# Products of constants placed in TensorE's waits at the two expert stages' seams

## What is computed

```python
def hierarchical_moe(h, ...):            # 4 groups of 8 experts, the 2 best of the best group
    glog = xf @ w_group + b_group
    g = argmax(glog)
    vals, loc = top_k(elog_g, 2)
    ...
    hb = silu(xb @ w_gate[e]) * (xb @ w_up[e])     # 1024 -> 512, per expert
    return hb @ w_down[e]                          # 512 -> 1024
```

## Time and profile before

| | us |
|---|---|
| median of 3 runs | 1779.08 (1778.0 to 1780.77) |
| the profiled execution's own time | 1777.53 |
| its span, first to last instruction | 1775.6 |
| TensorE busy | 1513.4 (85%), mean granted clock 0.918 |
| VectorE, ScalarE, GpSimd busy | 931.6, 167.4, 111.5 |
| read from HBM | 531.62 MB, 303 GB/s over the span |

### The profile page before, as it was taken

How to read it: one execution, slowest core, us unless ns; L and a number is a source line. 1 busy time by engine, 2 the same in 40 slices (tenths; PEclk the granted TensorE clock), 3 DMA queues, 4 the chain that set the end, 5 groups by cost and what they waited for, 6 DMA issues and landing times. The chain is left out here.

```text
span 1775.6 us, 33411 instructions
## 1 busy us (share of the span) xinstructions
PE 1513.4 (85%) x14935; PEld 1023.3 (58%) x14935; DVE 931.6 (52%) x1904; ACT 167.4 (9%) x389; POOL 111.5 (6%) x120
## 2 busy tenths in 40 slices
PE   8999967787777999776666666789999999999998
PEld 6655534454444995443333333589699446779843
DVE  6754344533235775344212221398867563886756
ACT  3210010000000101000100000111100003400000
POOL 2000100000000530000000000070000001000000
PEclk9999988888888999898878888799999999999999
DMA  9489999999999959999999999925355434345420
GB/s 315 185 322 425 391 417 426 426 426 426 427 426 409 377 210 367 426 422 428 426 427 427 426 428 426 395 95 206 139 190 190 141 123 157 125 142 191 150 88 24
DMA packets 80845, 540.11 MB, mean 304 GB/s; under 512 B 7454, under 2 KB 9566, under 8 KB 54332
## 3 DMA queue, kind: packets, MB, share of 16 engines
q1 hardware_dynamic: 78860, 531.18, 74.3%
q0 software_dynamic: 1808, 6.69, 1.0%
q10 hardware_dynamic: 32, 0.07, 0.0%
HBM read 531.62 MB, written 6.29 MB: 303 GB/s over the span
## 5 line engine op out<-in xcount | busy, mean ns | idle before, releaser
L973 PE MATMUL ps<-ring,work 128*32 128x256 f32 x3584 | 298.9, 506 | 207.4 <-DMA ring<-in_moe_w_up 206.9
L973 PEld LDWEIGHTS ps<-ring,work 128*32 128x32 f32 x3584 | 163.1, 144 | 338.1 <-issue 310.0
L2190 DVE TENSOR_TENSOR rowb<-rowb,ps 128x128 f32<-128x128 f32 x64 | 18.4, 287 | 354.0 <-ACT rowb L1857 353.9
L949 PE MATMUL ps<-ring,work 128*128 128x512 f32 x312 | 139.5, 592 | 0.0
L993 PE MATMUL ps<-ring,multi 128*32 128x256 f32 x1920 | 116.7, 383 | 0.3 <-DMA ring<-in_moe_w_down 0.2
L949 PEld LDWEIGHTS ps<-ring,work 128*128 128x128 f32 x312 | 59.0, 190 | 72.7 <-issue 72.7
L1550 PE MATMUL ps<-hT,ring 128*128 128x128 f32 x768 | 95.4, 275 | 1.5 <-ACT hT L1771 1.5
L949 PE MATMUL ps<-work 128*128 128x512 f32 x212 | 96.0, 592 | 0.0
L1550 PEld LDWEIGHTS ps<-hT,ring 128*128 128x128 f32 x768 | 90.4, 192 | 1.9 <-ACT hT L1771 1.9
L993 PEld LDWEIGHTS ps<-ring,multi 128*32 128x32 f32 x1920 | 62.8, 111 | 43.2 <-issue 2.9
L1014 PE MATMUL ps<-hres,rowb 128*32 128x256 f32 (+1 forms) x1240 | 84.5, 386 | 1.2 <-DVE rowb L2157 1.1
(11 more groups left out here) (624 smaller groups left out, 2268.6 us busy)
## 6 DMA issues: line engine op xcount, KB each, us to landing
ring<-in_moe_w_up SPq DMA_DIRECT2D x62, 2048.0 KB, 23.3
ring<-in_moe_w_gate SPq DMA_DIRECT2D x60, 2048.0 KB, 18.8
ring<-in_moe_w_down SPq DMA_DIRECT2D x58, 2048.0 KB, 24.0
ring<-in_w_ff SPq DMA_DIRECT2D x32, 2048.0 KB, 8.7
ring<-in_sc_w_in SPq DMA_DIRECT2D x6, 2048.0 KB, 22.3
ring<-in_ssm_w_glu SPq DMA_DIRECT2D x4, 2048.0 KB, 17.9
ring<-in_lru_w_in SPq DMA_DIRECT2D x3, 2048.0 KB, 17.6
ring<-in_lru_w_out SPq DMA_DIRECT2D x2, 2048.0 KB, 21.7
```

What stands on the lines that cost most here:

```text
L949: mm = pe.matmul(ps[:, product_bank[n][i], :], left[:, k, :], right[:, k, :], start=(j == 0 and k == 0), stop=(j == pieces - 1 and k == 1))
L973: mm = pe.matmul(ps[32 * q:32 * q + 32, bank, 0:256].rearrange("p (u n) -> p u n", u=2), x[:, k, :], gu[:, k, :, P * q:P * q + P], start=( ...
L2190: link(V.tensor_tensor(hid[b], silu[b], ps[:, 4 + b, P:2 * P], ALU.mult))
```

## The change

`keep_busy` takes a count of columns (288 before) and a bank (5 before). Two calls of 128 columns are added between ranks and picks in both layers; four calls in bank 7 stand between the last expert's gate and up products in layer 1; behind the last combination there are three calls in layer 0 (none before) and five in layer 1 (one before); one call follows the meta tokens' sum (L1366) and one the transposes of block 1 ahead of the wait for `ffn1_taken`. Nothing is removed or moved, and no other engine's program changes.

```diff
-            def keep_busy(n):
+            def keep_busy(n, cols=288, bank=5):
 
                 for _ in range(n):
-                    pe.matmul(ps[:, 5, 0:288], before[:, :], w_route[:, 1, :, :].rearrange("p k n -> p (k n)"), start=True, stop=True)
+                    pe.matmul(ps[:, bank, 0:cols], before[:, :], w_route[:, 1, :, :].rearrange("p k n -> p (k n)")[:, 0:cols],
+                              start=True, stop=True)
...
                 running_ranks(ps[:, 4, 384:384 + nb], tmp_a[:, 64:64 + nb], 1)
+                keep_busy(2, 128)
                 pe.wait_ge(*nth(f"one_hots{l}", 1))
...
                             gate_or_up(xT[b], 4 + b, gu, 0).then_inc(S(f"gate_up{l}"), 1)
+                            if l == 1:
+                                keep_busy(4, bank=7)
                         if gate_ is not None:
...
                 pe.end_ifs()
-                if l == 1:
-                    keep_busy(1)
+                keep_busy((3, 5)[l])
...
             pe.matmul(ps[:, 4, 0:NTAIL], ones[:, :], meta_acc[:, 0, :], start=True, stop=True).then_inc(S("meta_summed"), 1)
+            keep_busy(1)
...
                 transposes("ffn1", [1, 2], "ffn1_normed", only=i, bank=6, left="ffn1_left" if i == 0 else None)
                 if i == 0:
+                    keep_busy(1)
                     pe.wait_ge(*nth("ffn1_taken", 2))
                 s5_inputs(i)
```

## The result

The changed kernel takes **1782.6** against 1778.86 for the kernel before beside it (medians of 10 runs each), a ratio of 1.0024 [1.0016, 1.0032]. A second measurement on another occasion gave 1780.78 against 1778.33, 1.0012 [1.0003, 1.0022]. So it is slower by 2 to 4 us; forecast were 1774.8 and 4.3 gained.

What follows compares the result with a forecast made beforehand. Transfers bound both expert stages; outside them TensorE's lateness goes to the end whole. Gains of 4.06 (layer 1's seam), 0.25 (layer 0) and 0 (picks) sum to 4.3, from median 1779.08 to 1774.8 us; range 1772.6 to 1778.7.

Steps and rivals of the forecast that it cites:

- Five calls behind the last combination: Layer 1, ahead of the transposes: 2.65 us of calls fit in a wait of 4.19 and cost nothing at full clock.
- The clock term of 2.40: Layer 1, transposes to second L1439 group: the clock holds, adding 2.40 us, so the gain grows from 1.66 to 4.06.
- the weakest point: Layer 1, between transposes and L1439: idle 1.5, then 1.7 us, with only 1.6 of products between; the clock must hold.
- rival 1: Clock falls again between layer 1's transposes and L1439: only 1.9 to 3.0 us gained, 1776.1 to 1777.2; chance 0.30.
- The 1.66 ahead of the up products: Layer 1's last up products at full clock; the down matrix's second half, landing late, limits the seam's gain to 1.66 us.
- Layer 0 (0.25): Calls behind layer 0's combination and L1366: 0.25 us gained, at most 0.3, as the third unit's transfer limits it.
- 1.6 in a wait of 2.26: Three calls behind layer 0's last combination: 1.6 us of products hidden in a wait of 2.26.
- The picks (0): Two calls of 128 columns between ranks and picks: 0.5 us of products, hardly delaying the picks; gain taken as 0.
- the bounds of 0 and 1.15: Layer 1's picks: gain between 0 and 1.15 us, the latter if picks take 1.0 instead of 1.93.
- The one on the slow side: Fillers themselves late behind layer 1's last combination and ahead of its up products, if the clock at 1120 is 0.50; chance 0.05.
- the five: The five rivals: clock falls again, picks' filler holds the clock, layer 0 turns against it, fillers late, nothing holds.
- a lucky one: The profiled execution of the kernel before took 1777.53 us, 1.55 under the median of 1779.08.

Runs made afterwards that it cites:

- e9: e7 plus nine calls in the body of layer 1's branch, which is never taken, so every executed product is the same; 1780.83 us, ratio 1.0011.
- e13: The changed kernel without the branch in TensorE's program, all its calls in place; 1777.17 us, ratio 0.9997 to the kernel before.
- e4: The changed kernel with its three and five calls moved from behind the branch to ahead of it; 1777.58 us, ratio 0.9996 to the kernel before.
- e5: e4 without the two calls of 128 columns between ranks and picks; 1776.64 us, ratio 0.9991 to the kernel before.
- e16: e5 measured once more, nothing changed; 1777.05 us, ratio 0.9998 to the kernel before.
- e7: The kernel before with three and five calls behind the branch (before: none and one) as the only change; 1778.48 us, ratio 1.0004.
- e8: The kernel before with three and five calls ahead of the branch and none behind it as the only change; 1778.24 us, ratio 1.0002.
- e6: The kernel before plus only the two calls of 128 columns between ranks and picks; 1778.96 us, ratio 1.0002.
- e10: The changed kernel plus 52 calls inside layer 1's branch, never taken; 1782.36 us, ratio 1.002 to the kernel before.
- e2: The changed kernel with the calls behind the branch as before (none in layer 0, one in layer 1); 1778.64 us, ratio 1.0003 to the kernel before.
- e3: The changed kernel without the two calls of 128 columns between ranks and picks; 1780.49 us, ratio 1.0013 to the kernel before.
- e12: The changed kernel measured once more, nothing changed; 1780.78 us, ratio 1.0012 to the kernel before.
- e11: The kernel before plus twelve calls inside layer 1's branch, never taken; 1779.56 us, ratio 1.0006.
- e15: e5 without the four calls ahead of layer 1's last up products; 1777.78 us, ratio 0.9998 to the kernel before.
- e1: The kernel before plus only the four calls between layer 1's last gate and up products; 1778.08 us, ratio 0.9995.

## Why the prediction was wrong

**The step that failed** is "Five calls behind the last combination ... they cost nothing at full clock". I asked when the wait ends and how long the calls take, and took for granted that they start when the combination ends. They started 4.18 later, 2.56 behind the start of a packet of code: by my reading the code behind the branch was not there. The kernel before has such packets at both places too, with 0.94 lost ahead of L1366 in layer 0 and no idle time put down to issue in layer 1; the change did two things there: its other additions moved the edge, as counted, ahead of the calls, and its calls stood ahead of the transposes. Shown by e9 (edge moved, nothing else: the stall moves, +2.50 in the profiles and +2.35 in the medians), e13 (branch away: 3.6 to 5.4 less) and e4 (calls moved: 3 to 5 less).

**The clock term of 2.40 was right in kind and size.** From the first L1439 group to the second it was 6.38 before; forecast were 3.98, and it is 3.77 in the changed kernel and in e4, 3.78 in e13. With the calls in time, c falls from 17.85 by 1.65 (e4, e5, e16) to 2.59 (e13), and L1439's first group takes 2.01, as I had it (granted clock 1.00 in the changed kernel, 1147.7 to 1149.7). It needs more than the five calls: in e7 and e8, which have a stall among the transposes and no call behind them, that group took 3.55 and 3.80. Even in the changed kernel it worked: b is 5.3 longer than before and c only 1.2. Of the 4.1 that came back, 2.6 lie behind the start of L1439; the rest lies ahead of it, where the transposes took 1.04 for 1.94 and VectorE was no longer waited for. I called the place between transposes and L1439 the weakest point; rival 1 (the clock falls there again) did not come in any profile with all the calls.

**The 1.66 ahead of the up products was a term of one execution.** I took the down matrix's second half to land 5.0 behind the up matrix, from the one profile that I had. After the change it was 6.43 (issued at 1107.23, 26.4 to landing), and in 12 of the 17 profiles since, this one among them, its products start 6.3 to 6.5 behind the up products'. With that, slow products end just as it lands (first sixteen down products started 5.59 behind and took 1.0), and there is nothing to gain: a is 8.05 to 8.98 with fast up products in these, 8.22 before. Where it landed earlier, there was: 7.52 in e4 (5.90 behind), and 6.58 in e13 (4.96 behind), where my working has 6.56 (1129.26 and 1.04 make 1130.30 there, not 1130.33). So the step is right and its landing was mis-sized. What is worse, behind the longer wait of 2.2 the combination is slow (2.09 for 1.15).

**Layer 0 (0.25) was lost.** "1.6 in a wait of 2.26" rested on a wait of which 0.94 lay behind its releaser's end and ended 2.63 behind the start of a packet of code. The calls started at 574.63 and took 2.75 for the 1.6 that I had priced, and the block 2 transposes came 17.84 behind the last combination against 16.82. In the second profile of the changed kernel it was 16.63, so this term is less than one execution differs from another.

**The picks (0) hold for the whole (e6: 1.0002), but the bounds of 0 and 1.15 were wrong.** The four products cost 1.20 and 1.04 in the two profiles of the changed kernel and 0.69 in e6 and e10. From the first ranks to the second it is 7.23 before, 8.85 and 7.20 in the two profiles of the changed kernel, and 6.38 both in e6 with the calls and in e7 and e8 without. I left out that the calls could be the first to run slow. The clock differs between the two profiles of the changed kernel, 8.85 and 7.20: in the three stretches of 2 us from 696 on it was 1.00, 0.51 and 0.50 in the first and 0.88, 0.50 and 0.77 in the second.

**The rivals.** The one on the slow side (0.4 and 0.8 for the calls at half the clock and 1.3 in layer 0, so 1781.6) was near in time and had one of its places right, behind the last combination, but not the mechanism: the clock at 1120 was not 0.50 (the gate products at 1122.48 took 1.93), and the calls there did no harm. None of the five had TensorE's own program as the thing that is late. The row for it was there: a start 0.94 after its releaser's end.

**What stays open.** Of the 2 to 4 us, the stall ahead of layer 1's calls carries some 2.4 by e9 against e7, a figure that the noise leaves wide. The rest is not told apart: e2 and e3 differ from the changed kernel's two measurements by 2.1 to 4.0 and 0.3 to 2.1. That before's profile was "a lucky one" I had written; that the very row that I built 1.66 on was an unusual one, I had not seen.

## What to carry to other kernels

Put fillers, and all work that should start at once, ahead of a branch rather than behind it: with the same products there e4 was 3 to 5 under the changed kernel, and its calls ran from 1135.70 to 1140.58 while the packet of code started at 1137.55. Where a start comes later than its releaser's end, look for a packet of code that started 2.35 to 2.63 ahead of it, as in every stall here, and count the instructions between branch and stall before adding anything ahead: by the counts above each added product moved that place by 4. A term that rests on the distance of two landings needs more than one execution.

## What the runs showed of the hardware

- Behind the branch over the loop for tokens beyond the slots TensorE stood idle with no releaser for 1.6 to 2.3 us ahead of layer 0's calls (e3, e7, e9, e12 and the changed kernel; 0.27 in e10) and for 0.7 to 5.6 in layer 1 (the same, e2, e8, e10, e11, e15), with transfers at 388 GB/s beside it (changed kernel, 1137 to 1147). Without the branch (e13) no such idle time shows at either place.
- From the start of the packet of code to the first instruction beyond the edge it took 2.62 to 2.63 in layer 0 (the kernel before and after, e2, e3, e7, e9 to e12, e15) and 2.35 to 2.58 in layer 1 (the changed kernel, e2, e3, e7 to e12, e15).
- Code that never runs moved a stall from the middle of the transposes to ahead of the calls, and the median with it by 2.35 (e9 against e7).
- Behind a wait of 1.7 to 2.3 in the last down products the combination took 2.09 in the changed kernel (granted clock 0.50 from 1135.3 to 1137.4), e1 to e5, e10, e12 and e16; behind one of 0.75 to 0.88 it took 1.15 in e6 to e9 and e13 to e15 (1.00 from 1134.1 to 1135.3 in e13).
